# A larger ring of weights in the place of the scratch for GpSimd's transfers

## The chip, the cores and the metric

The kernel runs on one core of a Trainium2 chip. The core has TensorE (PE) for matrix products, VectorE (DVE), ScalarE (ACT) and GpSimd (POOL) for the rest, and SyncE (SP), which here issues the transfers. Weights come from HBM into SBUF, the memory of 128 partitions that the engines read; products go to PSUM. The metric is the time of one execution on the device, in microseconds (us).

## The reference, cut to what matters

Two blocks of two layers each work on 256 tokens of width 1024, all in float32. Each layer is a mixer followed by a mixture of experts. Three of the mixers are attention of one kind or another, the first is a gated MLP beside attention to a memory. The experts are what the change is about:

```python
def hierarchical_moe(h, w_group, b_group, w_expert, b_expert, w_gate, w_up, w_down):
    ...                                   # choice of a group, and of the top two experts in it
    weights = g_w * top_w
    combine = jnp.sum(jax.nn.one_hot(expert_id, N_EXPERTS, dtype=jnp.float32) * weights[..., None], axis=1)
    ...
        gate = jnp.einsum('td,edf->tef', xb, w_gate)
        up = jnp.einsum('td,edf->tef', xb, w_up)
        act = jax.nn.silu(gate) * up * cb[..., None].astype(xb.dtype)
        return jnp.einsum('tef,efd->td', act, w_down)
```

The first two layers have 32 experts, the last two 16, each with 1024 x 256 weights for gate, up and down. `first_block` and `second_block` call this after each mixer, and the second block also scales and shifts by a modulation that is computed from a vector with the weights `w_ada_2`.

## The kernel before, in words

**The ring.** Nearly all weights pass once through one tile, `ring`, of RING columns of float32 (12 MB over the 128 partitions). The whole list of chunks is fixed when the program is built: `Stream.add` gives every chunk its place, wrapping to column 0 where the rest is too short, and works out `need`, the number of earlier chunks that must be used up before it may be overwritten; with LOADS = 16 semaphores for landings, a chunk may also not be issued before the one 16 ahead of it is used. The gate, up and down weights of an expert are three pieces of PIECE = 2048 columns, 1 MB each; those of the dense layers are chunks of 2 or 3 MB, and the 16 chunks of `w_ada_2`, 3 MB each, are spread between them.

**Who fills it.** SyncE alone issues the ring's transfers, in the order of the list (line 96, `Stream.issue`). Each of them waits for `chunk_used`, which the engine that last reads a chunk raises. A block of the program issues what can be freed within it, so the ring runs ahead of the products by as much as it holds. Between them SyncE issues loads that have tiles of their own: the down weights of the first experts of a stage (`first_down`, `half_down`, `hT`, `late_down`, parts of `catT` and `mem_kv`), rows, biases and the router's weights.

**An expert stage (`moe`).** Tokens are sorted by expert with products, and each expert's tokens are taken in a window of 32 slots. Experts are taken in pairs. For a pair i, TensorE computes gate and up in two halves of k (line 1671, 32 products of 128 x 512 each), then the products with the down weights (line 1694), and adds the weighed rows of the pair before (line 1717). GpSimd copies the windows (line 1564), ScalarE applies Silu and frees the ring's pieces (lines 1866, 1868 and 1847), VectorE multiplies and weighs. The order of the ring's pieces is that of `expert_pieces`: gate and up of a pair, then the down weights of the pair before. The down weights of the first 5, 6, 4 and 4 experts (ASIDE) are not in the ring. TensorE waits for a piece where it is first read.

**The general path.** If some expert has more than 32 tokens in one half, every engine branches to code that computes all experts for all tokens (`every_token`). There the combine weights are stored to DRAM and read back, one row per expert, broadcast over the partitions into `cb`.
Of the kernel before, what the change touches and what calls it, by code (L numbers as in the profile page):

```python
# [22 lines left out]
P = 128  # L23
T = 256
# [2 lines left out]
KT = D // P  # L27
EPS = 1e-6
NEG = -1e30
RING = 4 * 6144  # L30
LOADS = 16
FF = 256
PIECE = 2048
# [88 lines left out]
def build(nc, A, out, stop=99):  # L122
    ctx = ExitStack()
    with ctx:
        def sem(name):
            return ctx.enter_context(nc.semaphore(name))
# [3 lines left out]
        def sig(name):  # L130
            if name not in names:
                names[name] = Signal(sem(name))
            return names[name]
# [3 lines left out]
        def sbuf(stack, name, shape, dt=F32):  # L137
            uniq[0] += 1
            return stack.enter_context(nc.sbuf_tensor(f"{name}_{uniq[0]}", shape, dt))
# [12 lines left out]
        PS = ctx.enter_context(nc.psum_tensor("PS", [P, 8, BANK], F32))  # L152
        ring = sbuf(ctx, "ring", [P, RING])
        chunk_used = sem("chunk_used")
# [1205 lines left out]
        def moe(m, first, E, gain, shift, gate, then):  # L1360
# [7 lines left out]
            with ExitStack() as st:  # L1368
# [73 lines left out]
                cb = flat[:, 3072:4096].rearrange("p (j t) -> p j t", j=4)  # L1442
                combT = flat[0:E, 4096:4096 + T]
# [14 lines left out]
                ct_ready, ct_sb, c_stored = sig("combT_ready"), sig("combT_taken"), sig("comb_stored")  # L1458
                gate_ready, up_ready, silu_ready = sig("gate_ready"), sig("up_ready"), sig("silu_ready")
                hid_ready, up_taken = sig("hid_ready"), sig("up_taken")  # L1460
# [7 lines left out]
                cb_loaded = [sig(f"cb_loaded{j}") for j in range(4)]  # L1468
# [51 lines left out]
                def _(pool):  # L1520
# [23 lines left out]
                    def every_token(pool):  # L1544

                        pool.wait_ge(*ct_sb.at(1))
                        nc.gpsimd.dma_start(A["comb_dram"][0:E, :], combT).then_inc(c_stored.sem, 16)
                        pool.wait_ge(*c_stored.at(16))
                        for e in range(E):
                            if e >= 4:  # L1550
                                pool.wait_ge(*up_taken.at(e - 3))
                            nc.gpsimd.dma_start(cb[:, e % 4, :], A["comb_dram"][e:e + 1, :].to_broadcast([P, T])).then_inc(cb_loaded[e % 4].sem, 16)
                        nc.gpsimd.sem_inc(win_ready.sem, 2 * E + 4)

                    far_from_here("gpsimd", f"rows_{m}", block.end_bb, every_token)
                    nc.gpsimd.br_cond(fits(nc.gpsimd) > 0, on_true=f"slots_{m}", on_false=f"rows_{m}")
                    nc.switch_bb(f"slots_{m}")
# [238 lines left out]
                def _(act):  # L1796
# [22 lines left out]
                    def take_ranks_and_weights(act):  # L1819

                        act.wait_ge(*rank_rows.at(1))
                        nc.scalar.copy(ranks, PS[:, 0, 0:T]).then_inc(rank_rows_taken.sem, 1)
                        act.wait_ge(*weight_rows.at(1))
                        nc.scalar.copy(weights, PS[:, 1, 0:T]).then_inc(weight_rows_taken.sem, 1)

                    act.wait_ge(*table_ready.at(1))
                    def every_token(act):

                        take_ranks_and_weights(act)
                        act.wait_ge(*ct_ready.at(1))  # L1830
                        nc.scalar.copy(combT, PS[0:E, 4, 0:T]).then_inc(ct_sb.sem, 1)
                        for e in range(E):
                            act.wait_ge(*gate_ready.at(e + 1))
                            if e >= 2:
                                act.wait_ge(*hid_ready.at(e - 1))
                            nc.scalar.activation(sg[:, e % 2, :], PS[:, 4 + e % 2, :], ACT.Silu).then_inc(silu_ready.sem, 1)
                        nc.scalar.sem_inc(y_high.sem, highs)

                    far_from_here("scalar", f"every_silu_{m}", f"rejoin_act_{m}", every_token)
                    before_branch = nc.cur_bb  # L1840
                    nc.scalar.br_cond(fits(nc.scalar) > 0, on_true=f"silu_{m}", on_false=f"every_silu_{m}")
# [1449 lines left out]
```

## Time and profile before

| | |
|---|---|
| Runs | 1534.68, 1537.2, 1545.22 us; median 1537.2 |
| Profiled execution, its span | 1536.0 us, of 23584 instructions |
| TensorE busy | 1432.1 us, 93% |
| VectorE, ScalarE, GpSimd busy | 737.2, 495.9, 102.6 us |
| Read from HBM | 465.42 MB, 305 GB/s over the span |
| First expert stage, last product pair | 191.6 to 404 us |
| Second | 591.1 to 804 us |
| Third, fourth | 1169.5 to 1266 us, 1432.4 to 1528 us |

The profile is of one execution other than the three that were timed; its span, from the first to the last instruction, is 1.2 us below the median of those. The page is that of the one core. The stretches of the expert stages are read from the timeline of lines 1671 and 1694. The transfers are far from even: 42 to 426 GB/s in the page's 40 slices of 38.4 us.

### The profile page before, as it was taken

To read this page: it belongs to the slowest core of one execution; us is meant where nothing else is said; L and a number is where in the kernel's file an instruction comes from. 1 tells how busy PE (TensorE), PEld (TensorE's weight loads), DVE (VectorE), ACT (ScalarE), POOL (GpSimd) and SP (SyncE) were. 2 spreads that over 40 slices of the span, in tenths; PEclk is the share of its full clock that TensorE was granted. 3 is DMA by queue.
4 is the path that set the end of the run, shared out by engine and by line. 5 is a ranking of instruction groups with operands and counts; after the bars stand their busy time and mean duration, and the time that the engine had idled before them with its cause. 6 is when DMAs were issued, how large, how long until landed. Compare 5 with 4: busy or idle time off the path is not lost. (4 is left out here: it accounts for less than half of the span.)

```text
span 1536.0 us, 23584 instructions
## 1 busy us (share of the span) xinstructions
PE 1432.1 (93%) x9090; PEld 786.3 (51%) x9090; DVE 737.2 (48%) x1659; ACT 495.9 (32%) x996; POOL 102.6 (7%) x258
## 2 busy tenths in 40 slices
PE   7999999987899899998888998999899998989998
PEld 4585533322365644332227876788655336765432
DVE  1467432222255544222226755675585346668534
ACT  3231211111226412111116656565512116661211
POOL 0000011100000001110102000200001102000110
PEclk9999999999999999999999999999898999999999
DMA  8798799999963189999997462335169996437997
GB/s 358 313 365 334 294 381 417 421 420 422 426 266 145 59 336 386 398 422 420 421 424 302 165 225 77 110 143 227 42 230 422 420 425 248 174 156 301 422 420 299
DMA packets 63399, 469.78 MB, mean 306 GB/s; under 512 B 7809, under 2 KB 15921, under 8 KB 18738
## 3 DMA queue, kind: packets, MB, share of 16 engines
q1 hardware_dynamic: 63282, 468.22, 75.2%
q8 instruction: 74, 1.21, 0.3%
q14 instruction: 43, 0.35, 0.1%
HBM read 465.42 MB, written 2.76 MB: 305 GB/s over the span
## 5 line engine op out<-in xcount | busy, mean ns | idle before, releaser
L1671 PE MATMUL PS<-ring,catT 128*32 128x512 f32 x3072 | 348.0, 594 | 18.8 <-issue 16.4
L826 PE MATMUL PS<-w_split,h_split 128*128 128x512 f32 x1152 | 272.7, 396 | 6.0 <-DVE w_split L911 6.0
L826 PEld LDWEIGHTS PS<-w_split,h_split 128*128 128x128 f32 x1152 | 215.5, 190 | 56.9 <-DVE w_split L911 8.5
L1671 PEld LDWEIGHTS PS<-ring,catT 128*32 128x32 f32 x3072 | 96.4, 110 | 235.0 <-issue 234.8
L911 DVE TENSOR_TENSOR w_split<-ring,w_split 128x512 fp32r<-128x512 f32 x192 | 132.6, 705 | 69.3 <-ACT w_split L859 68.7
L1694 PE MATMUL PS<-ring,row_place 128*32 128x512 f32 x1232 | 142.3, 593 | 20.2 <-issue 20.1
L859 ACT CAST w_split<-ring 128x512 fp32r<-128x512 f32 x192 | 118.0, 619 | 106.7 <-PE PS L826 106.2
L1869 ACT ACTIVATE row_place<-PS 128x256 f32<-128x256 f32 x48 | 18.4, 384 | 367.7 <-PE PS L1671 367.7
L1694 PEld LDWEIGHTS PS<-ring,row_place 128*32 128x32 f32 x1232 | 41.4, 110 | 112.1 <-issue 112.1
L508 PE MATMUL PS<-ring,catT 128*128 128x512 f32 x224 | 96.7, 592 | 1.0 <-PEq L1022 1.0
L1564 POOL COPY catT<-xsT 128x256 f32 x176 | 63.3, 404 | 405.4 <-PE PS L1671 397.8
L2054 DVE TENSOR_TENSOR row_place<-PS,row_place 128x256 f32<-128x256 f32 x48 | 20.3, 422 | 132.3 <-ACT row_place L1869 132.3
L2058 DVE COPY row_place<-PS 128x256 f32<-128x256 f32 x48 | 20.4, 424 | 117.4 <-PE PS L1680 117.4
L508 PEld LDWEIGHTS PS<-ring,catT 128*128 128x128 f32 x224 | 42.3, 190 | 53.3 <-issue 53.3
L438 DVE CUSTOM_DVE_ANT_0 ring<-ring,row_place 128x1024 f32<-128x1024 f32 x48 | 55.6, 1223 | 8.5 <-DMA row_place<-silu_dram 5.5
L2079 DVE SCALAR_TENSOR_TENSOR gated_rows<-PS,slot_w,grow 128x512 f32<-128x512 f32 x32 | 24.0, 750 | 68.3 <-PE PS L1694 68.1
L2086 DVE SCALAR_TENSOR_TENSOR xn_split<-PS,slot_w,xn_split 128x512 fp32r<-128x512 f32 x36 | 27.0, 751 | 52.2 <-ACT xn_split L1856 52.2
L1538 POOL MEMSET xsT<- 128x512 f32 x4 | 2.1, 526 | 638.0 <-POOLq L476 510.4
L2601 PE MATMUL PS<-ring,catT 128*128 128x512 f32 x96 | 41.7, 594 | 1.1 <-DVE catT L2493 0.9
L1856 ACT ACTIVATE xn_split<-PS,slot_w 128x512 fp32r<-128x512 f32 x36 | 24.7, 687 | 54.6 <-PE PS L1694 54.6
L438 DVE CUSTOM_DVE_ANT_0 ring<-ring,silu_row 128x1024 f32<-128x1024 f32 x36 | 41.7, 1220 | 1.3 <-PE PS L2400 1.3
L2086 DVE SCALAR_TENSOR_TENSOR xn_low_rows<-PS,slot_w,xn_low_rows 128x512 fp32r<-128x512 f32 x26 | 19.5, 751 | 43.5 <-ACT xn_low_rows L1856 43.5
(445 smaller groups left out, 1869.2 us busy)
## 6 DMA issues: line engine op xcount, KB each, us to landing
ring<-in_moe SPq DMA_DIRECT2D x269, 1024.0 KB, 15.2
ring<-in_w_ada SPq DMA_DIRECT2D x16, 3072.0 KB, 12.2
ring<-in_a_w_in SPq DMA_DIRECT2D x23, 2048.0 KB, 14.4
ring<-in_b_w_in SPq DMA_DIRECT2D x8, 2048.0 KB, 20.1
first_down<-in_moe SPq DMA_DIRECT2D x8, 1024.0 KB, 8.5
ring<-in_a_w_out SPq DMA_DIRECT2D x2, 3072.0 KB, 18.3
ring<-in_b_w_out SPq DMA_DIRECT2D x2, 3072.0 KB, 13.9
ring<-in_w_mem_kv SPq DMA_DIRECT2D x2, 2048.0 KB, 11.5
```

The lines of the kernel that those rows point to most:

```text
L438: last = nc.vector.tensor_tensor_reduce(w[:, m, :], w[:, m, :], row, 1.0, 0.0, ALU.mult, ALU.add, ada_out[:, 6 * c + m:6 * c + m + 1])
L508: last = nc.tensor.matmul(PS[:, i % 8, 0:n], srcT[:, j, t * P:(t + 1) * P], w[:, j, o:o + n], start=j == 0, stop=j == k - 1)
L826: last = nc.tensor.matmul(PS[:, 2 * (i % 2) + t, :], hs[:, hp, k, t * P:(t + 1) * P], wk[:, (KT * i + k) % splits, wp, :], start=k == 0 an ...
L859: nc.scalar.copy(wk[:, (KT * i + k) % splits, 0, :], w[:, k, :]).then_inc(w_high.sem, 1)
L911: nc.vector.tensor_tensor(wk[:, (KT * i + k) % splits, 1, :], w[:, k, :], wk[:, (KT * i + k) % splits, 0, :].bitcast(F32), ALU.subtract).t ...
L1564: nc.gpsimd.tensor_copy(xf[:, i % 2, :, q * HALF:(q + 1) * HALF], padded(q // 2)[:, :, bass.ds(at, HALF)]).then_inc(win_ready.sem, 1)
L1671: last = nc.tensor.matmul(PS[lanes, 4 + i % 2, :].rearrange("p (g f) -> p g f", g=2), xf[:, i % 2, k, lanes], gate_up_weights(2 * i + q % ...
L1694: last = nc.tensor.matmul(PS[lanes, 6 + c, :], hs[:, i % 2, f2, lanes], down_weights(2 * i + q % 2, f2)[:, c * BANK:(c + 1) * BANK], start ...
L1856: nc.scalar.activation(yk(i, 0, c), PS[:, 6 + c, :], ACT.Copy, scale=slot_w[:, i % 2, :]).then_inc(y_high.sem, 1)
L2079: nc.vector.scalar_tensor_tensor(gated[:, c, :], PS[:, 6 + c, :], slot_w[:, i % 2, :], grow[:, c * BANK:(c + 1) * BANK], ALU.mult, ALU.mul ...
L2086: nc.vector.scalar_tensor_tensor(yk(i, 1, c), PS[:, 6 + c, :], slot_w[:, i % 2, :], high, ALU.mult, ALU.subtract).then_inc(y_low.sem, 1)
L2601: last = nc.tensor.matmul(PS[:, bank, :], catT[:, k, t * P:(t + 1) * P], w[:, k, :], start=n == 0, stop=n == 11)
```

## The change

RING grows from 4 x 6144 = 24576 columns to 14 x 2048 = 28672, from 12 to 14 MB. The 16 KB per partition come from the scratch of GpSimd's transfers, which is cut to 64 bytes, and GpSimd issues no transfer any more: the general path's store and its E loads are issued by ScalarE, within its loop over the experts and with the same waits. The ring began at byte 16512 of each partition and begins at byte 192; all tiles behind it move up by 64 bytes.

```diff
--- before.py
+++ after.py
@@ -27,7 +27,7 @@
 KT = D // P
 EPS = 1e-6
 NEG = -1e30
-RING = 4 * 6144
+RING = 14 * 2048
 LOADS = 16
 FF = 256
 PIECE = 2048
@@ -1544,12 +1544,6 @@
                     def every_token(pool):
 
                         pool.wait_ge(*ct_sb.at(1))
-                        nc.gpsimd.dma_start(A["comb_dram"][0:E, :], combT).then_inc(c_stored.sem, 16)
-                        pool.wait_ge(*c_stored.at(16))
-                        for e in range(E):
-                            if e >= 4:
-                                pool.wait_ge(*up_taken.at(e - 3))
-                            nc.gpsimd.dma_start(cb[:, e % 4, :], A["comb_dram"][e:e + 1, :].to_broadcast([P, T])).then_inc(cb_loaded[e % 4].sem, 16)
                         nc.gpsimd.sem_inc(win_ready.sem, 2 * E + 4)
 
                     far_from_here("gpsimd", f"rows_{m}", block.end_bb, every_token)
@@ -1829,7 +1823,13 @@
                         take_ranks_and_weights(act)
                         act.wait_ge(*ct_ready.at(1))
                         nc.scalar.copy(combT, PS[0:E, 4, 0:T]).then_inc(ct_sb.sem, 1)
+                        act.wait_ge(*ct_sb.at(1))
+                        nc.scalar.dma_start(A["comb_dram"][0:E, :], combT).then_inc(c_stored.sem, 16)
+                        act.wait_ge(*c_stored.at(16))
                         for e in range(E):
+                            if e >= 4:
+                                act.wait_ge(*up_taken.at(e - 3))
+                            nc.scalar.dma_start(cb[:, e % 4, :], A["comb_dram"][e:e + 1, :].to_broadcast([P, T])).then_inc(cb_loaded[e % 4].sem, 16)
                             act.wait_ge(*gate_ready.at(e + 1))
                             if e >= 2:
                                 act.wait_ge(*hid_ready.at(e - 1))
@@ -3269,7 +3269,7 @@
     feeds["slot_no"] = np.arange(S2).astype(np.float32)
     feeds["desc"] = np.arange(32, 0, -1).astype(np.float32)
 
-    nc = bacc.Bacc("TRN2", target_bir_lowering=False, num_devices=1)
+    nc = bacc.Bacc("TRN2", target_bir_lowering=False, num_devices=1, dynamic_dma_scratch_size=64)
     A = {"col_at": col_at}
     arrays = {}
     for name, v in feeds.items():
```

The ring's places and needs are worked out when the program is built, so the diff doesn't show what moves. SyncE's queue does. (Rows are: line, operation, destination tile <- source, shape, count; UNCONDITIONAL_BRANCH ends a block; L96 is a transfer into the ring.) Around the start of the first expert stage, the block ahead of it:

```order
@@ -39,5 +39,5 @@
 L254 DMA half_down<-in_moe 128x1024
 L96 DMA ring<-in_a_w_out 128x6144
-L96 DMA ring<-in_moe 128x2048 x12
+L96 DMA ring<-in_moe 128x2048 x14
 L2509 UNCONDITIONAL_BRANCH
 L1502 UNCONDITIONAL_BRANCH
```

and, in the stage itself, behind its own loads:

```order
@@ -45,5 +45,5 @@
 L1508 DMA hT<-in_moe 128x2048
 L1510 DMA late_down<-in_moe 128x2048
-L96 DMA ring<-in_moe 128x2048 x79
+L96 DMA ring<-in_moe 128x2048 x77
 L96 DMA ring<-in_b_w_in 128x4096
 L96 DMA ring<-in_w_ada 128x6144
```

Two pieces of the stage's experts moved from behind the loads of `hT` and `late_down` to ahead of the stage. Around the start of the second expert stage, first the end of the block of the second mixer (L2723), then the block of its output projection:

```order
@@ -58,4 +58,6 @@
 L96 DMA ring<-in_w_ada 128x6144
 L96 DMA ring<-in_b_w_out 128x6144 x2
+L96 DMA ring<-in_w_ada 128x6144
+L96 DMA ring<-in_moe 128x2048
 L2723 UNCONDITIONAL_BRANCH
 L477 UNCONDITIONAL_BRANCH
```

```order
@@ -66,6 +68,5 @@
 L254 DMA half_down<-in_moe 128x1024
 L256 DMA mem_kv<-in_moe 128x2048
-L96 DMA ring<-in_w_ada 128x6144
-L96 DMA ring<-in_moe 128x2048 x6
+L96 DMA ring<-in_moe 128x2048 x7
 L476 UNCONDITIONAL_BRANCH
 L1502 UNCONDITIONAL_BRANCH
```

A 3 MB chunk of `w_ada_2` and the first piece of the experts moved ahead of that projection and of the loads that it begins with; seven pieces follow where six did. The projection ahead of the third expert stage:

```order
@@ -109,23 +109,21 @@
 L485 DMA catT<-in_br 128x20
 L248 DMA first_down<-in_moe 128x2048 x2
-L96 DMA ring<-in_w_ada 128x6144
-L96 DMA ring<-in_moe 128x2048 x2
+L96 DMA ring<-in_moe 128x2048 x6
 L476 UNCONDITIONAL_BRANCH
 L1502 UNCONDITIONAL_BRANCH
-L96 DMA ring<-in_moe 128x2048 x10
+L96 DMA ring<-in_moe 128x2048 x8
 L1508 DMA hT<-in_moe 128x2048
 L1510 DMA late_down<-in_moe 128x2048
-L96 DMA ring<-in_moe 128x2048 x32
+L96 DMA ring<-in_moe 128x2048 x30
 L96 DMA ring<-in_b_w_in 128x4096 x3
 L96 DMA ring<-in_b_w_in 128x128
-L96 DMA ring<-in_b_w_in 128x4096 x2
+L96 DMA ring<-in_b_w_in 128x4096 x3
 L1368 UNCONDITIONAL_BRANCH
 L776 UNCONDITIONAL_BRANCH
-L96 DMA ring<-in_b_w_in 128x4096
 L96 DMA ring<-in_w_ada 128x6144
+L96 DMA ring<-in_b_w_out 128x4096 x2
 L3164 DMA cum_dram<-grow 16x256
 L3167 DMA key_bias<-cum_dram 128x1024 x4
-L96 DMA ring<-in_b_w_out 128x4096 x2
-L96 DMA ring<-in_w_ada 128x6144
+L96 DMA ring<-in_w_ada 128x6144 x2
 L751 UNCONDITIONAL_BRANCH
 L477 UNCONDITIONAL_BRANCH
```

Here too a chunk of `w_ada_2` went to an earlier block, and six pieces of the experts are issued in the place of two.

## Rows read from the trace of the kernel before

**Rows 1.** The page, parts 1 and 2: TensorE's busy time; GB/s by slice.
```profile
PE 1432.1 (93%) x9090; PEld 786.3 (51%) x9090; DVE 737.2 (48%) x1659; ACT 495.9 (32%) x996; POOL 102.6 (7%) x258
...
GB/s 358 313 365 334 294 381 417 421 420 422 426 266 145 59 336 386 398 422 420 421 424 302 165 225 77 110 143 227 42 230 422 420 425 248 174 156 301 422 420 299
```

**Rows 2.** Groups by line, PE, 196 to 300 us: busy and mean | idle before.
```profile
L1671 PE MATMUL PS<-ring,catT 128*32 128x512 f32 x584 | 66.2, 594 | 0.0
L1694 PE MATMUL PS<-ring,row_place 128*32 128x512 f32 x176 | 21.7, 592 | 0.0
```

**Rows 3.** Groups by line, PE, 300 to 400 us.
```profile
L1671 PE MATMUL PS<-ring,catT 128*32 128x512 f32 x412 | 46.9, 594 | 9.4 <-issue 8.5 <-DMA ring<-in_moe 0.9
L1694 PE MATMUL PS<-ring,row_place 128*32 128x512 f32 x226 | 26.3, 595 | 9.5 <-issue 9.5
```

**Rows 4.** Groups by line, PE, 700 to 800 us.
```profile
L1671 PE MATMUL PS<-ring,catT 128*32 128x512 f32 x408 | 46.4, 594 | 9.3 <-issue 7.9 <-DMA ring<-in_moe 1.4
L1694 PE MATMUL PS<-ring,row_place 128*32 128x512 f32 x232 | 26.8, 595 | 9.5 <-issue 9.5
```

**Rows 5.** Stretches: length, busy by engine (x), PEclk, DMA share, GB/s.
```profile
135.00:141.00 6.00, 6.00 (x15) 2.65 (x14) 5.85 (x12) 0.23 (x1) 0.00 (x0) 1.00 1.04 428
185.00:196.00 11.00, 10.84 (x90) 6.54 (x90) 9.39 (x32) 4.94 (x11) 3.36 (x12) 1.00 0.28 95
196.00:300.00 104.00, 104.00 (x928) 33.65 (x928) 29.32 (x74) 15.10 (x27) 13.46 (x38) 1.00 1.00 410
300.00:400.00 100.00, 81.12 (x700) 26.36 (x693) 21.48 (x51) 12.30 (x21) 7.18 (x20) 1.00 1.01 422
430.00:530.00 100.00, 93.33 (x423) 63.80 (x423) 58.61 (x146) 48.07 (x136) 0.00 (x0) 0.98 0.37 148
700.00:800.00 100.00, 81.18 (x702) 26.46 (x698) 21.93 (x52) 12.31 (x21) 7.19 (x20) 1.00 1.01 422
1177.00:1182.00 5.00, 5.00 (x50) 1.45 (x46) 0.82 (x3) 0.38 (x1) 1.44 (x4) 1.00 1.02 418
```

**Rows 6.** Timeline, PE, 270 to 345 us: start, length, what [idle before].
```profile
275.22 3.64 PE L1671 MATMUL PS<-ring,catT 128*32 128x512 f32 x32
...
287.16 3.64 PE L1671 MATMUL PS<-ring,catT 128*32 128x512 f32 x32
...
314.05 3.64 PE L1671 MATMUL PS<-ring,catT 128*32 128x512 f32 x32
...
328.99 3.64 PE L1671 MATMUL PS<-ring,catT 128*32 128x512 f32 x32
```

**Rows 7.** The page, part 6: issues, KB each, us to landing.
```profile
ring<-in_moe SPq DMA_DIRECT2D x269, 1024.0 KB, 15.2
```

**Rows 8.** Timeline, SP queue, 164 to 197 us.
```profile
169.88 1.28 SPq L96 DMA_DIRECT2D ring<-in_moe  x3
...
178.46 0.33 SPq L1508 DMA_DIRECT2D hT<-in_moe  x1
191.73 0.33 SPq L1510 DMA_DIRECT2D late_down<-in_moe  x1
196.39 1.42 SPq L96 DMA_DIRECT2D ring<-in_moe  x2
```

**Rows 9.** Timeline, PE, ends of the third and fourth expert stages.
```profile
1253.10 3.64 PE L1671 MATMUL PS<-ring,catT 128*32 128x512 f32 x32
...
1261.75 3.64 PE L1694 MATMUL PS<-ring,row_place 128*32 128x512 f32 x32 [0.81 <-issue]
...
1515.94 3.64 PE L1671 MATMUL PS<-ring,catT 128*32 128x512 f32 x32
...
1523.86 3.64 PE L1694 MATMUL PS<-ring,row_place 128*32 128x512 f32 x32 [0.33 <-issue]
```

**Rows 10.** Waits of the SP queue: total us, times, longest.
```profile
SPq L2723 <- PEq L2723: 26.3, 1, 26.3
```

**Rows 11.** The page, part 5: GpSimd's copies of windows.
```profile
L1564 POOL COPY catT<-xsT 128x256 f32 x176 | 63.3, 404 | 405.4 <-PE PS L1671 397.8
```

## The prediction

> **What bounds the kernel now.** I read the page first, for the whole span: TensorE is busy for 1432.1 of 1536.0 us, and the row of GB/s says that the transfers run in bursts, 420 and more in some slices, 42 to 145 in others [rows 1]. So there is no single bound, and the change has to be priced stage by stage. The two kinds of bursts that matter are the expert stages, where every expert's weights (3 pieces of 1 MB) pass through the ring.
>
> The groups by line for two halves of the first expert stage come next. From 196 to 300 us the products of gate and up (L1671) and of the down weights (L1694) have 0.0 us of idle time before them [rows 2]; from 300 to 400 us the same two lines have 9.4 + 9.5 = 18.9 us of it [rows 3]. The second expert stage repeats this: 9.3 + 9.5 = 18.8 us from 700 to 800 us [rows 4]. The table by stretch shows what runs meanwhile: from 300 to 400 us the DMA share is 1.01 at 422 GB/s and TensorE is busy for 81.12 of 100 us, from 700 to 800 us 81.18 of 100 [rows 5]. The rows name "issue" as the releaser for most of this, but the period gives the cause away. A pair of experts takes TensorE 287.16 - 275.22 = 11.94 us while nothing is missing, and 328.99 - 314.05 = 14.94 us later [rows 6]. A piece is 1024 KB [rows 7], 1.0486 MB; at 422 GB/s that is 2.485 us, and the six pieces of a pair take 14.9 us. That is the late period: in the second half TensorE waits for weights.
>
> The picture is thus a race. TensorE eats a pair in 11.94 us, the transfers bring one in 14.9 us, and the stage starts with a full ring of 12 pieces as a head start. It lasts until about 300 us; from then to the end of the stage the last piece's landing sets the time.
>
> **What the change does to the race.** The ring holds 14 pieces. The rows of the order show it for SyncE: 14 pieces of the first expert stage stand ahead of that stage's other work where 12 stood, and 77 behind where 79 stood; for the second stage one piece moves into an earlier block, 7 + 6 instead of 6 + 6 follow, and 76 stand behind where 78 stood.
>
> Step 1: are the two more pieces there in time? They cost 2 x 2.485 = 4.97 us of transfer, ahead of the stage. Before the first stage SyncE issues three ring pieces at 169.88 us and then none until 196.39 us, when the first slot comes free [rows 8]; from 185 to 196 us the DMA share is 0.28 [rows 5], that is 0.72 x 11 = 7.9 us of idle transfer time, and 4.97 fits. Before the second stage the share is 0.37 in the 100 us from 430 to 530 us, into which the order moves one 3 MB and one 1 MB transfer [rows 5]. So yes, in both.
>
> Step 2: does the later stream keep its pace? A slot is freed by the same products at the same times while TensorE does not wait, so piece n+2 goes out when piece n did, and everything that the stage brings lands two pieces, 4.97 us, earlier. TensorE has 18.9 and 18.8 us of such waiting to give back, more than 4.97, so the whole of it comes through: **4.97 us in each of the two long stages, 9.94 together**. Nothing downstream takes it back: the transfers of the next stage follow in the same queue and move up by the same 4.97 us.
>
> Step 3: the two short expert stages (16 experts). Here the head start lasts almost to the end. From the start of the last gate and up half to the start of the last down products it is 1261.75 - 1253.10 = 8.65 us in the third, 1523.86 - 1515.94 = 7.92 us in the fourth, with a last wait of 0.81 and 0.33 us [rows 9]. The third gives back at least the 0.73 us by which it is the longer, at most 1.04 with the 0.33 that the fourth waits too; the fourth gives 0 to 0.33. I take 0.9 and 0.1, since a chain through ScalarE and VectorE stands before those products in any case: **1.0 us**.
>
> Step 4: what is moved past what. SyncE's queue is in order. In the block of the second mixer it now waits for a further slot before it reaches the block's end; it stood there for 26.3 us before the others came [rows 10], so 0. In the first expert stage the load for `hT` and the one for `late_down` go out at 178.46 and 191.73 us [rows 8], now behind up to 4.97 us more of transfers; the products that read `hT` are the second pair's down products, behind a whole pair of 11.94 us, and those that read `late_down` one pair later, so 0. Before the third stage a 3 MB load of `w_ada_2` moves ahead of its block; VectorE had hardly waited for it: 0, at most a few tenths gained.
>
> Step 5: the general path. It does not run here: GpSimd's copies of windows, x176 in L1564, are those of the short path [rows 11]. The 1 + E transfers that move to ScalarE cost nothing, and neither does the lost scratch, as no transfer of this execution is issued by GpSimd. If an input did take that path, ScalarE would wait for a store and for `up_taken` ahead of its Silu; no row prices that.
>
> **The sum.** 4.97 + 4.97 + 1.0 = 10.9 us. The profiled execution spans 1536.0 us, so its successor spans 1525.1. The median of the three runs, 1537.2, lies 1.2 us above that span, and what surrounds it is not touched: **1526.3 us**, 0.7% less. The bounds of the terms give 9.9 to 11.3 us, 1525.9 to 1527.3.
>
> The price of a piece deserves a second look, as all hangs on it: the row gives 422 GB/s [rows 5], hence 2.485 us. The Trainium skill, "DMA: Bandwidth & Descriptors", Specifications, lists a limit of about 358 GB/s for one core's share of HBM; by that (an estimate from the page) a piece would take 2.93 us and the sum would be 12.7 us, 1524.5. The measured rate decides, and it is above that limit.
>
> **Rivals.**
>
> *The dips go too (faster).* In the first halves of the long stages the rate is 410 GB/s, not 422 [rows 5]. Should the deeper ring close that, it is worth (1 - 410/422) x 104 = 3.0 us in each, some 5.7 more: 1520.6. Against it: the rate dips where all free slots have been filled, and slots come free at TensorE's pace whatever the ring's size. Chance 0.07.
>
> *Part of the head start does not come through.* A piece may land late, or the chain behind the products may already be the bound once waits are shorter. Then one piece's worth or nothing is gained in each stage: 1531 to 1537. Against it: the 7.9 us of idle time, and 0.0 us of idle in [rows 2]. Chance 0.10.
>
> *The transfers get slower (the other side).* The ring moves in SBUF: it began at byte 16512 of a partition (128 above a multiple of 256) and now begins at byte 192 (192 above one), and all tiles behind it shift by 64 bytes. In a long stage 77 pieces, 191 us, follow the first free slot; a rate lower by 2.6% eats the 4.97 us, and anything above makes the kernel slower. At 7% each long stage would lose 13.4 - 5.0 = 8.4 us, 1554. Against it: from 135 to 141 us, when mostly `first_down` and `half_down` are filled (both 160 above a multiple of 256), the rate is 428 GB/s, no less than in the ring [rows 5]. Chance 0.03.
>
> *A mild form of it.* From 1177 to 1182 us, when the third stage's `hT` and `late_down` are filled, the rate is 418 GB/s, 1% below 422 [rows 5]. If the ring fell to that, each long stage would lose 1.9 us: 1526.3 + 3.8 = 1530.1. Chance 0.08, for the same reason. The Trainium skill, "DMA: Bandwidth & Descriptors", section "How a descriptor splits into AXI transactions", has a rule of that size: an estimate from it is that a row of 8192 bytes starting 128 above a boundary of 256 costs 260 beats and one starting 192 above it 262, 0.8% more, if the written side follows it too. By that rule the time would be 1529.4; the 428 GB/s of the other tiles speaks against it so far.
>
> *The ring does not grow in effect.* 16 semaphores count the landings, and a piece may be issued only when that of 16 before is used. 14 pieces stay below that, and the order shows them ahead of the stage. I give it no chance.
>
> **Chances and range.** Forecast 0.72, the rivals 0.07, 0.10, 0.03, 0.08. I call 1% what a measurement can tell from no change; 1% of 1537.2 is 15.4 us. Faster by more needs the dips to go, or a favourable spread: 0.09. Slower by more is the strong form of the third rival: 0.03. Within 1%: 0.88. The runs of before spread from 1534.68 to 1545.22, so the median itself may sit 2 or 3 us off; with the first rival below and the mild one and half of the second above, the range is 1520 to 1533.
>
> **What would show it.** In the changed kernel's trace: SyncE's issues ahead of the first expert stage x14; the first long stage's waits in L1671 and L1694 begin one to two pairs later than 300 us and sum to about 14 us instead of 19; the pair's late period stays 14.9 us and the rate 422 GB/s; the last down products of that stage start 5 us earlier against its own start; from the last gate and up half to the last down products the third stage takes 7.9 us or less. I am wrong if the rate in the late halves is not 421 to 423 GB/s, if the head start's two pieces land after the stage's first slot comes free, or if the stages between gain or lose more than 1 us.

## The result, and the profile after

The first four runs of the changed kernel took 1514.16, 1522.96, 1509.48 and 1518.09 us, median 1516.12; the ratio to the kernel before is 0.9887 [0.9851, 0.9924]. Six more runs beside other kernels gave 1512.75 us and 0.9863 [0.9837, 0.9888]. So the change makes the kernel 1.1 to 1.4% faster, 17 to 21 us; 10.9 us were forecast, and 1516.12 lies below the range of 1520 to 1533. Two executions far above the others, one of 1849.55 us of the kernel before and one of 3552.27 us of e1 below, are left out throughout as slow ones.

The profiled execution spans 1512.4 us, 23.6 us less than the one before. First its page: busy times, granted clock and transfer rate in 40 slices, and the issues of ring pieces. They answer to [rows 1, 7].

```profile
span 1512.4 us, 23584 instructions
PE 1419.4 (94%) x9090; PEld 776.4 (51%) x9090; DVE 736.8 (49%) x1659; ACT 495.6 (33%) x996; POOL 102.5 (7%) x258
...
PEclk9999999999999999999999999999899999999999
...
GB/s 360 362 346 254 419 343 413 420 421 420 427 300 188 112 279 419 402 421 420 420 425 285 187 291 44 111 158 221 68 261 421 420 423 300 173 107 302 421 419 239
...
ring<-in_moe SPq DMA_DIRECT2D x269, 1024.0 KB, 13.8
```

The work is the same; TensorE's busy time fell by 12.7 us although it does the same products. That can't come from waits that are gone, and the mean granted clock of the execution, in the view of the cores, says what it is, before and after.

```profile
core: us from the first to the last instruction, mean granted TensorE clock
core 0: 1536.0 us, clock 0.975
```
```profile
core: us from the first to the last instruction, mean granted TensorE clock
core 0: 1512.4 us, clock 0.985
```

Next the waits, as groups by line of PE over the whole of the first long stage (192 to 399 us) and of the second (581 to 786 us), after. The columns are those of [rows 2].

```profile
L1665 PE MATMUL PS<-ring,catT 128*32 128x512 f32 x1024 | 116.1, 594 | 6.8 <-issue 6.1 <-DMA ring<-in_moe 0.7
L1688 PE MATMUL PS<-ring,row_place 128*32 128x512 f32 x432 | 51.0, 593 | 6.9 <-issue 6.9
...
L1665 PE MATMUL PS<-ring,catT 128*32 128x512 f32 x1024 | 116.0, 594 | 6.2 <-issue 5.3 <-DMA ring<-in_moe 0.9
L1688 PE MATMUL PS<-ring,row_place 128*32 128x512 f32 x416 | 47.4, 593 | 6.3 <-issue 6.3
```

The waits sum to 13.7 and 12.5 us, where 18.9 and 18.8 stood [rows 3, 4]. The stages themselves, from the first product of gate and up to the last down product, stand in the tables by stretch: before, then after, then the three stretches between the stages of either. The columns are those of [rows 5].

```profile
191.63:403.62 211.99, 193.11 (x1699) 62.89 (x1698) 56.05 (x142) 30.16 (x53) 22.64 (x64) 1.00 1.00 413
591.14:803.14 212.00, 193.18 (x1699) 62.95 (x1698) 55.70 (x142) 30.16 (x53) 22.64 (x64) 1.00 1.00 411
1169.53:1265.39 95.86, 95.00 (x850) 30.73 (x850) 38.09 (x95) 15.14 (x29) 11.13 (x32) 1.00 1.02 422
1432.39:1527.49 95.10, 94.76 (x850) 30.74 (x850) 37.83 (x95) 15.16 (x29) 11.18 (x32) 1.00 0.96 397
403.62:591.14 187.52, 177.97 (x713) 109.40 (x711) 95.57 (x234) 65.77 (x171) 1.90 (x6) 0.96 0.59 241
803.14:1169.53 366.39, 341.52 (x1826) 267.14 (x1826) 234.91 (x443) 198.54 (x379) 17.51 (x22) 0.94 0.48 183
1265.39:1432.39 167.00, 155.05 (x785) 109.63 (x786) 121.34 (x303) 89.33 (x194) 9.63 (x14) 0.96 0.59 236
```
```profile
192.40:398.48 206.08, 192.42 (x1699) 62.64 (x1698) 56.00 (x142) 30.17 (x53) 22.59 (x64) 1.00 1.00 412
581.06:785.83 204.77, 192.23 (x1699) 62.48 (x1698) 55.66 (x142) 30.16 (x53) 22.60 (x64) 1.00 1.01 417
1148.99:1243.57 94.58, 94.58 (x850) 30.66 (x850) 37.82 (x94) 15.00 (x29) 11.12 (x32) 1.00 1.01 421
1408.34:1502.92 94.58, 94.58 (x850) 30.66 (x850) 37.86 (x94) 15.01 (x29) 11.11 (x32) 1.00 0.91 378
398.48:581.06 182.58, 171.28 (x711) 104.58 (x711) 95.51 (x234) 65.65 (x171) 1.89 (x6) 1.00 0.62 255
785.83:1148.99 363.16, 338.62 (x1826) 264.19 (x1826) 234.63 (x443) 198.49 (x379) 17.57 (x22) 0.95 0.52 196
1243.57:1408.34 164.77, 152.84 (x786) 108.17 (x786) 121.51 (x303) 89.33 (x195) 9.74 (x14) 0.98 0.60 237
```

The four stages give 5.9, 7.2, 1.3 and 0.5 us, 14.9 together. Between them 4.9, 3.2 and 2.2 us more are gone, with the granted clock (the seventh column) up from 0.96 to 1.00, from 0.94 to 0.95 and from 0.96 to 0.98. It is busy time alone that fell there: TensorE stands idle for 9.55, 24.87 and 11.95 us before and for 11.30, 24.54 and 11.93 after. Two questions follow: how much of 14.9 us is the ring and how much the luck of two executions, and why the clock is higher.

The steps that need only the trace: from 300 to 398 us and from 685 to 785 us the rate is as it was [rows 5], and the late pairs keep their period (319.31 to 334.51 is 15.2 us, with one landing 0.3 us late in it), here from the timeline of PE.

```profile
300.00:398.00 98.00, 84.34 (x734) 27.32 (x726) 22.91 (x54) 13.00 (x22) 7.16 (x20) 1.00 1.02 422
...
685.00:785.00 100.00, 87.46 (x760) 28.64 (x756) 24.00 (x59) 13.01 (x22) 7.16 (x20) 1.00 1.01 422
```
```profile
319.31 3.64 PE L1665 MATMUL PS<-ring,catT 128*32 128x512 f32 x32 [0.47 <-issue]
...
334.51 3.64 PE L1665 MATMUL PS<-ring,catT 128*32 128x512 f32 x32 [1.64 <-issue]
```

### The profile page after: what moved, and what is told of

It reads as the page before. It is cut to its first block and busy times, and to the rows that moved or that the text cites. A ratio compares the mean times of both kernels' runs of the same rounds, so it can differ in the third digit from the quotient of the medians.

```text
span 1512.4 us, 23584 instructions
## 1 busy us (share of the span) xinstructions
PE 1419.4 (94%) x9090; PEld 776.4 (51%) x9090; DVE 736.8 (49%) x1659; ACT 495.6 (33%) x996; POOL 102.5 (7%) x258
## 5 line engine op out<-in xcount | busy, mean ns | idle before, releaser
L1869 ACT ACTIVATE row_place<-PS 128x256 f32<-128x256 f32 x48 | 18.5, 384 | 361.1 <-PE PS L1665 361.1
L791 POOL TENSOR_TENSOR h_split<-hT,h_split 128x256 fp32r<-128x256 f32 x24 | 23.7, 995 | 235.8 <-ACT h_split L869 233.1
## 6 DMA issues: line engine op xcount, KB each, us to landing
ring<-in_a_w_in SPq DMA_DIRECT2D x23, 2048.0 KB, 10.9
ring<-in_w_mem_kv SPq DMA_DIRECT2D x2, 2048.0 KB, 11.3
```

## The experiments

Two figures are used throughout. A kernel's **mean granted clock** is the mean over its timed runs. Its time **at equal clock** is from one straight line through 186 runs of 15 kernels (all but the ring of 10 pieces), with a level of its own for each: 10.3 us (standard error 0.5) per 0.01 of clock, read at 0.980. It leaves 2.1 us of scatter where the plain times of one kernel scatter by 2 to 6.

### Only the depth, undone and in steps

```diff
-RING = 14 * 2048
+RING = 12 * 2048        # e1; 13 * 2048 in e2, 10 * 2048 in e4
```

> The changed kernel with its ring back at 12 pieces: the missing scratch, the ring's new address and ScalarE's issues stay, and only the depth is undone. Theory, the depth is all of it: the four expert stages are as long as in the kernel before (212.0, 212.0, 95.9 and 95.1 us, within 1 us of the landing stalls' scatter), and the ratio to the kernel before is 0.998 to 1.002. Rival, the layout does something (address or scratch): the ratio stays below 0.995 and transfers in the late halves are faster than 2.485 us a piece. Rival, the clock: the part of the difference outside the expert stages (8.7 us of 23.6 in the two profiled executions, nine stretches of low granted clock instead of thirteen) is scatter; then this kernel's executions show both kinds of profile, low ones near 9 and near 13.

Measured: 1535.34 us, ratio 0.9995 [0.9966, 1.0023]. The address of the ring, the missing scratch and ScalarE's issues do nothing that these runs can tell (0.3% at most); the depth is all of it. This falsifies both rivals of slower transfers as well: the ring lies at its new place here too, and the time at equal clock is 1533.7 us, that of the kernel before. The clock was 0.9795, that of the kernel before (0.9792 in 75 runs), and its trace has twelve low stretches: the clock did not rise with the rest of the change.

> A ring of 13 pieces, all else as in the changed kernel. Theory, depth: one piece of 2.485 us in each long stage, so about 209.5 us for each, and in the third stage nearly all of what 14 give (94.6 to 95.0 us); the ratio lies halfway between that of 12 and of 14 pieces, about 0.995. Rival, something that comes with the change as a whole and not per piece: the ratio is that of 14 pieces, 0.989, or that of 12.

Measured: 1528.57 us, ratio 0.9952 [0.9925, 0.9979]; at equal clock 1526.0 against 1533.7, so 7.7 us for the first piece and 7.0 for the second. The long stages took 208.41 and 209.72 us, as expected; the third 96.27, not 94.6 to 95.0, in this one execution. Its queue had issued the last burst 18.3 us ahead of that stage, and the piece for the first freed slot landed 18.0 us into it; the section on the third stage tells what that does.

```diff
+HELD = 12 * 2048
+            held = i
+            while held and sum(hi - lo for lo, hi in self.place[held - 1:]) <= HELD:
+                held -= 1
-            self.need.append(max([0, i - len(self.loaded) + 1, *self.need[-1:], *behind]))
+            self.need.append(max([0, i - len(self.loaded) + 1, *self.need[-1:], *behind, held]))
```

> The ring has 14 pieces of room, but a transfer is issued only while at most 12 pieces are in it. Theory, what counts is how many pieces are ahead of TensorE: long stages of 212 us, ratio to the kernel before 0.998 to 1.002, as with 12 pieces of room. Rival, what counts is that a slot is written later after it was read, or which addresses are written: ratio 0.989 as with 14.

Measured: 1529.56 us, ratio 0.9962 [0.9937, 0.9986]. The long stages took 211.56 and 211.12 us, so there the theory holds. But the two short ones took 94.58 us each, no wait in them, as with 14 pieces of room. That was not expected: the same 12 MB were worth more in a ring of 14. The stretch of its third stage:

```profile
1165.24:1259.82 94.58, 94.58 (x850) 30.66 (x850) 37.86 (x94) 15.00 (x29) 11.11 (x32) 1.00 1.01 421
```

The cause is in SyncE's rows ahead of the third stage, below.

> A ring of 10 pieces. Theory, depth: the waits begin two pairs earlier, each long stage takes 5.0 us more than with 12 pieces (217 us), and the two short ones, in which the head start of 12 just about lasts, take 4 to 5 us more each (about 100 us). Sum 18 to 20 us, ratio 1.012 to 1.013. Rival, there is a loss beside the head start as the ring shrinks (transfers between the stages come late too, as some stages keep 3 MB transfers in it): over 1.015. Rival, the head start is worth less than its bytes: under 1.008.

Measured: 1622.03 us, ratio 1.0584 [1.0540, 1.0627], a plain miss of the theory; the first rival, a loss beside the head start, had been put at over 1.015. The long stages took 215.65 and 214.66 us and the short ones 101.71 and 99.24, near the forecast, 19.0 us above e1 in all. The other 68 us were lost elsewhere. Against the trace of e1, 18.8 us of them lie ahead of the first stage and 9.9, 13.0 and 21.4 us between the stages; the granted clock was lower too, 0.9588 in the mean. A later kernel narrows down the reason:

> Room for 14 pieces, but the pieces of the expert stages are held at 10 in the ring; the 2 and 3 MB transfers of the other stages are free to use all 14. Theory, the 87 us that the ring of 10 pieces lost were not head start but the large transfers, which leave gaps at the end of a ring of 10 MB and wait for each other: here the parts between the expert stages are as long as with 12 (184 and 367 us, not 194 and 381), the long stages take 212 + 5 = 217 us, less what the ring of 10 showed (215 us), the short ones 99 to 101; ratio 1.006 to 1.012. Rival, the ring of 10 was slow because so few pieces are in flight in an expert stage: ratio above 1.03.

Here ring pieces of the expert stages are held at 10 as above, and nothing else. Measured: 1546.42 us, ratio 1.0099 [1.0062, 1.0137], with 215.5, 215.2, 98.7 and 100.3 us in the stages. The tables by stretch for the part between the first and second stage and for that between the second and third, the ring of 10 ahead of the held one:

```profile
426.74:620.88 194.14, 175.65 (x711) 106.96 (x711) 95.66 (x234) 65.83 (x172) 1.89 (x6) 0.96 0.55 222
835.54:1216.35 380.81, 339.65 (x1825) 265.49 (x1826) 235.28 (x443) 198.42 (x379) 17.59 (x22) 0.94 0.46 173
```
```profile
407.44:596.61 189.17, 177.94 (x710) 108.41 (x710) 95.51 (x234) 65.62 (x171) 1.90 (x6) 0.96 0.57 232
811.81:1171.33 359.52, 334.96 (x1825) 260.62 (x1826) 235.00 (x443) 198.52 (x379) 18.29 (x22) 0.96 0.50 187
```

With the room of 14 TensorE stands idle for 11.2 and 24.6 us in them, as in the other kernels (9.6 and 24.9 in e1, 11.3 and 24.5 after); in the ring of 10 for 18.5 and 41.2. So what the ring of 10 lacked was room for the transfers of the other stages, a second effect of a ring's size. That it is the way in which they fit (ten pieces hold three transfers of 3 MB and leave 1 MB unused), and not the smaller room as such, is inferred; no run separates the two. In the expert stages a piece less costs about what was forecast: 4.3 to 4.8 us for two in each long one.

### The third stage

The timeline of SyncE's queue ahead of the third stage, in the kernel before, in e3, and after:

```profile
1128.02 0.33 SPq L96 DMA_DIRECT2D ring<-in_w_ada  x1
1135.91 17.62 SPq L96 DMA_DIRECT2D ring<-in_moe  x12
...
1169.53 0.33 SPq L1510 DMA_DIRECT2D late_down<-in_moe  x1
```
```profile
1126.59 0.33 SPq L100 DMA_DIRECT2D ring<-in_w_ada  x1
1126.96 24.16 SPq L100 DMA_DIRECT2D ring<-in_moe  x12
...
1165.24 0.33 SPq L1514 DMA_DIRECT2D late_down<-in_moe  x1
```
```profile
1110.51 24.24 SPq L96 DMA_DIRECT2D ring<-in_moe  x14
...
1148.99 0.33 SPq L1510 DMA_DIRECT2D late_down<-in_moe  x1
```

`late_down` goes out as the stage begins. Before, the first piece goes out 33.6 us ahead of it, behind the 3 MB transfer of `w_ada_2`; in e3 38.3 us ahead, in the changed kernel 38.5. The output projection ahead of the stage begins at 1118.60, 1117.29 and 1101.10 us (its first product in the timeline of PE), and each queue goes on 9.3 to 9.4 us behind that. The ring of 12 then has room for the `w_ada_2` transfer alone, and the first piece goes out 7.9 us later; with 14 MB of room, in e3 as in the changed kernel, pieces go out at once. What they gain is transfer time, not only room. From the DMA rows of 50 us (40 before the stage, 10 of it; 40 slices) of the kernel before and after:

```profile
GB/s 157 413 393 452 452 367 190 406 426 426 197 20 0 13 0 26 203 413 419 439 426 426 433 419 419 433 419 419 419 419 419 426 419 433 426 413 433 419 419 406
```
```profile
GB/s 20 33 170 406 426 433 433 426 439 426 439 419 419 419 144 13 0 0 170 406 419 433 426 419 426 426 419 419 426 439 419 426 419 419 413 419 426 419 426 406
```

Before the pause both move weights; after it both are at the limit without a break into the stage. So this short stage is bound by transfers from the start on. The first slot comes free 4.8 us into every stage. In the long stages of the changed kernel the ring is full by then (its last piece landed 4.6 us ahead of the first stage and 1.8 us into the second); in the third stage of the kernel before it is not, its last piece landed 7.4 us into the stage. The piece for the first freed slot landed 15.3 us into the third stage before, 12.6 after and 12.5 in e3, against 10.5 us into the first stage before and 9.6 after. With 12 pieces the length of the third stage depends on how long ahead of it the burst behind the pause is issued. Two further traces with 12 pieces (e9 and e11, below) show what that does: third stages of 99.01 and 98.60 us. Its stretch by engine, and the stretch from the issue of the burst to the stage's start, e9; then the latter in the kernel before:

```profile
1159.30:1258.31 99.01, 95.42 (x850) 30.93 (x850) 38.09 (x95) 15.15 (x29) 11.08 (x32) 1.00 1.01 421
...
1141.48:1159.30 17.82, 17.74 (x114) 15.74 (x115) 15.13 (x50) 9.06 (x17) 1.79 (x6) 0.81 0.95 387
```
```profile
1148.48:1169.53 21.05, 20.96 (x114) 18.44 (x114) 14.85 (x50) 9.07 (x17) 1.81 (x6) 0.68 0.96 393
```

The same 114 products took 21.05 us at a clock of 0.68 and 17.82 at 0.81. The faster clock brings the stage 3.2 us nearer to the burst, and the stage gives 3.2 us back in waits (99.01 - 95.86). The other two traces agree: 21.1 us and a stage of 95.88 in e1, 18.3 us and 98.60 in e11, so that the two sum to 116.8 to 117.0 us in all four. With 14 pieces the third stage was 94.58 or 94.59 us in all six traces, whatever the clock ahead of it.

### What the waits of the long stages are

```diff
+            n = PIECE // 2 if self.raw(i).shape[1] == PIECE and i >= 29 else self.raw(i).shape[1]
-            nc.sync.dma_start(self.raw(i), self.chunks[i])
+            nc.sync.dma_start(self.raw(i)[:, 0:n], self.chunks[i][:, 0:n])
```

> The changed kernel in which the transfers of the expert stages bring half of each piece (from the 15th piece of the first stage on), so that half of the products read what was in the slot before; the number of transfers, waits and products is the same. Theory, the late waits are transfer time: all of TensorE's waits in the two long stages are gone (13.7 and 12.5 us), the stages take 192.4 us each, and the ratio to the kernel before is about 0.974 (1520 - 26 us). Rival, part of these waits is a chain through the other engines or the queue (a wait seen by TensorE, but not for bytes): the long stages stay above 196 us.

The kernel leaves out the second half of each piece, and the products read what lay in the slot before; it serves as a measurement alone. Measured: 1491.0 us, ratio 0.9724 [0.9690, 0.9757]; the long stages took 190.27 us each. The table by stretch:

```profile
194.20:384.47 190.27, 190.27 (x1699) 61.43 (x1698) 56.06 (x142) 30.12 (x53) 22.63 (x64) 1.00 0.76 258
566.42:756.69 190.27, 190.27 (x1699) 61.40 (x1698) 55.70 (x142) 30.14 (x53) 22.64 (x64) 1.00 0.76 265
```

No idle time is left, at the same number of transfers. The waits named "issue" were bytes, and 30.3 us are still in reach in the changed kernel's two long stages (206.08 + 204.77 - 2 x 190.27: 26.2 us of waits, the rest in what TensorE is busy around them).

### Where the higher clock comes from

> The changed kernel once more, unchanged, for a larger sample and a second trace. At equal granted clock the runs so far put 12 pieces of room at 1533.7 and 1534.3 us, 13 at 1526.0, and 14 at 1520.0 from four runs only. Theory, the rest was chance: the mean clock of twelve runs is 0.980 as in the other kernels (0.9837 in the four), the median is 1519 to 1521, the ratio 0.990 to 0.992, the long stages 206 to 207 us, and some of the low-clock stretches missing from the first trace are back. Rival, fewer waits raise the clock: the mean clock stays at 0.983 or more and the ratio at 0.989. Rival, the stalls in the early half of the second stage (4.5 to 5.9 us in three traces with 12 pieces, 4.8 with 13, 2.2 with 14) go with the deeper ring: they are about 2 us again; by chance alone they are back at 5.

Measured: 1512.75 us, ratio 0.9863 [0.9837, 0.9888], mean clock 0.9858. Chance as the cause of the higher clock falls: the ten runs of the changed kernel have 0.985 in the mean, and the 26 runs of 14 pieces other than e12 0.9847, against 0.9792 in 75 of the kernel before. (The stalls of the second stage's early half were 5.0 us again, against 2.2 in the first trace; here chance is at work.) "Fewer waits raise it" falls too, since e6 waits least of all and has 0.9778. The remaining runs move the program in time, with fillers on TensorE:

```diff
-                    keep_busy(3, 12)
+                    keep_busy(3, 12 + 8 if m == 0 else 12)    # e8, e9; 4 in e10, e11
+                    keep_busy(3, 12 + 8 if m == 2 else 12)    # e12; m == 1 in e13, e14 and, with 4, e15
```

> The changed kernel with eight more filler products of TensorE (0.21 us each, 1.7 us) ahead of the first expert stage's gathering products; everything behind them stands 1.7 us later. The ten runs of the changed kernel have a mean granted clock of 0.985, 39 runs of the kernel before 0.9797; that is 5 us of the difference. Theory, alignment: the low-clock stretches stand at the same places of the program in every trace, and whether each falls, and how long it is, depends on how the program's pauses lie in time; the 13 to 15 us by which 14 pieces move the later parts happen to suit them. Then a shift of 1.7 us changes the mean clock (down toward 0.980), and the time grows by more than 1.7 us. Rival, the clock is higher because TensorE's waits in the expert stages are fewer: the mean clock stays at 0.985, and the time grows by 1.7 us.

> The kernel before with the same eight filler products. Theory, alignment: its mean clock changes too, and since it is low (0.9797), more likely up than down, so that the time grows by less than 1.7 us or falls. Rival, waits: the clock stays at 0.980 and the ratio to the kernel before is 1.001.

> The changed kernel with four more filler products, 0.85 us. Theory, alignment: a mean clock between those of no shift and of 1.7 us, or outside both. Rival, waits: 0.985 and 0.85 us more than the changed kernel.

> The kernel before with four more filler products, 0.85 us. Theory, alignment: its mean clock differs from 0.9797 by more than its standard error. Rival, waits: it does not. At equal clock both shifted kernels of 12 pieces and both of 14 keep the distance of 14.8 us that the rows show so far.

> The changed kernel with eight more filler products (1.7 us) ahead of the third expert stage's gathering products, so that what lies behind that stage stands as late against the stage before it as with 12 pieces, whose third stage is 1.3 us or more longer. In all four traces of 14 pieces no stretch of low clock falls 95 us behind the third stage, in all four of 12 pieces one does. Theory, alignment: that stretch is back in the trace, the mean clock goes from 0.984 to 0.981 or below, and the time rises by 3 to 6 us. Rival, it goes with 14 pieces as such: clock 0.984, time 1.7 us more than the changed kernel (1514), the stretch stays absent.

> The changed kernel with the eight filler products ahead of the second expert stage. Theory, alignment: the landing stalls of the second stage scatter its end by about 1 us anyway, so that this shift does little, like the one ahead of the first stage: clock 0.983 to 0.985. Rival: the same clock; this run by itself only bounds how much a shift there can do.

> The kernel with half the bytes in the expert stages (half of the products read what was in the slot before), with eight more filler products ahead of the second expert stage. Theory, alignment: its clock, 0.977 to 0.980 in four runs, moves by more than 0.003 in one direction. Rival, the clock is set by what the kernel does and not by where it lies: 0.978 again, the time 1.7 us above the 1490 us without them.

> The same with four filler products (0.85 us). Theory, alignment: the clock differs from that with none and with eight. Rival: 0.978 again, the time 0.85 us above 1490 us.

| kernel | shift | median us | ratio | mean clock | at 0.980 |
|---|---|---|---|---|---|
| before (75 runs) | | | | 0.9792 | 1533.7 |
| e1, 12 pieces | none | 1535.34 | 0.9995 | 0.9795 | 1533.7 |
| e11, 12 pieces | 0.85 us, first stage | 1535.99 | 1.0004 [0.9978, 1.0029] | 0.9773 | 1533.7 |
| e9, 12 pieces | 1.7 us, first | 1537.29 | 1.0013 [0.9991, 1.0036] | 0.9791 | 1536.2 |
| changed, and e5 | none | 1516.12, 1512.75 | 0.9887, 0.9863 | 0.9837, 0.9858 | 1520.0, 1518.3 |
| e10, 14 pieces | 0.85 us, first | 1513.51 | 0.9866 [0.9834, 0.9897] | 0.9840 | 1518.6 |
| e8, 14 pieces | 1.7 us, first | 1516.16 | 0.9863 [0.9832, 0.9894] | 0.9842 | 1519.8 |
| e13, 14 pieces | 1.7 us, second | 1513.80 | 0.9861 [0.9828, 0.9893] | 0.9855 | 1520.0 |
| e12, 14 pieces | 1.7 us, third | 1522.01 | 0.9909 [0.9878, 0.9940] | 0.9795 | 1520.3 |
| e6, half bytes | none | 1491.0 | 0.9724 | 0.9778 | 1487.8 |
| e15, half bytes | 0.85 us, second | 1482.56 | 0.9660 [0.9629, 0.9691] | 0.9824 | 1486.6 |
| e14, half bytes | 1.7 us, second | 1486.15 | 0.9665 [0.9635, 0.9696] | 0.9814 | 1486.8 |

The shifts ahead of the first stage change the clock of neither ring, which is what the rival of the alignment theory had forecast for e8 to e11, and the one ahead of the second (e13) does nothing either. With the one ahead of the third stage the clock of 14 pieces is back at that of 12: 1.7 us of fillers there cost 7.0 us in the mean of eight runs (1520.9 against 1513.8). In the kernel with half the bytes the fillers go with a faster program, 1485.3 and 1484.1 us in the mean against 1490.1; these are five, five and four runs whose times overlap, so this is a hint and not a result.

One detail of the forecast failed, and it is the one that would have tied the loss to a place: in the trace of e12 (clock 0.981, one of its better runs) the stretch of low clock 95 us behind the third stage was not back. The part between the third and the fourth stage, in e1, after and e12:

```profile
1261.34:1428.40 167.06, 155.04 (x787) 109.70 (x787) 121.34 (x303) 89.31 (x194) 9.61 (x14) 0.96 0.60 237
...
1243.57:1408.34 164.77, 152.84 (x786) 108.17 (x786) 121.51 (x303) 89.33 (x195) 9.74 (x14) 0.98 0.60 237
...
1247.11:1411.56 164.45, 151.68 (x786) 107.03 (x786) 121.49 (x303) 89.34 (x195) 9.62 (x14) 0.98 0.59 237
```

This part took 164.4 to 164.9 us in all six traces with 14 pieces and 167.0 to 172.8 in the four with 12: 4.0 us in the mean. The part between the second and the third stage gives another 4.0 (364.6 against 360.6, e12 with its fillers aside). But that between the first and the second took 185.6 us in the mean with 12 and 184.9 with 14 (e13 aside), so most of the 4.9 us that the two profiled executions differ by there was luck. What is shown, then, is that the higher clock comes with the depth (e1 has all else), that fewer waits are not what raises it (e6), and that a shift ahead of the third stage takes it away. That it depends on how the late parts lie in time is the reading that fits these best; no trace shows where e12 lost its 7 us.

That stretch shows the dependence best. By table of stretches, the 8 us ahead of it and its 3.4 us, before and after:

```profile
1353.00:1361.00 8.00, 5.51 (x42) 3.02 (x42) 4.64 (x27) 5.35 (x18) 0.00 (x0) 1.00 0.60 257
1361.00:1364.40 3.40, 3.40 (x19) 2.00 (x17) 1.84 (x11) 2.50 (x11) 0.00 (x0) 0.50 0.01 2
```
```profile
1331.00:1339.00 8.00, 5.58 (x46) 3.39 (x46) 5.33 (x31) 5.58 (x19) 0.00 (x0) 1.00 0.80 343
1339.00:1342.40 3.40, 3.40 (x32) 2.13 (x30) 3.11 (x20) 3.40 (x12) 0.00 (x0) 1.00 0.01 2
```

Same place, same products, the same two pauses of 1.03 and 1.46 us ahead of it (the stretches of after are set 0.7 us later against the second pause, hence the other counts in the first of the two); before, 2.4 GHz fell to 1.2 for 3.4 us, 0.3 us behind that pause, and after it did not. What exactly decides it I leave open; it was not isolated further than by the shifts.

## Why the prediction was wrong, step by step

**The forecast's time fails by three terms**; the mechanism, its steps 1, 2 and 5, stands.

*The price per piece in the long stages* (4.97 us each): right. Four traces with 12 pieces in effect (before, e1, e9, e11) have 211.1 and 211.4 us in the mean, six with 14 (after, e5, e8, e10, e12, e13) 206.5 and 205.3: 4.6 and 6.0 us, 10.7 for the 9.94 forecast. A single late landing is worth about 1 us and there are several in each stage, so the 5.9 and 7.2 us of the two profiled executions were partly luck. The pieces were there in time (the last of the 14 landed 4.6 us ahead of the first stage, and the piece for the first freed slot 9.6 us into it, 10.5 before), the late rate is 422 GB/s, and the first wait of the first stage comes 126.9 us into it instead of 112.4, a pair and a bit later.

*Step 3, the short stages* (1.0 us): wrong, and it is the term of the mechanism that failed. I read the third stage as one whose "head start lasts almost to the end", from one execution's last wait. In truth its transfers were behind from the start, and its waits were small only as a stretch of low clock had held the stage back. Over the same traces it took 97.3 us with 12 pieces and 94.6 with 14, the fourth 94.9 and 94.6: 2.7 + 0.3 = 3.0 us, not 1.0. The one trace of e3 has the whole gain of the third stage with 12 pieces held, so that it needs the room beside the 3 MB transfer and not 14 pieces ahead. The edit that step 4 put at nothing "or a few tenths", the 3 MB load of `w_ada_2` ahead of its block, belongs to this. The sign that I had named for it, 7.9 us or less from the last gate and up half to the last down half, was met (1232.56 to some 1239.9 us) and was too weak to tell 1.0 from 3.0. (Small sums of the forecast are off as well: 0.73 + 0.33 is 1.06 and not 1.04, its own least value of 0.73 puts the lower bound of the sum at 10.7 and not 9.9, and twice 3.0 is 5.9 or 6.0 and not 5.7. None of them matters here.)

The stages together give 10.7 + 3.0 = 13.7 us, and the comparison at equal clock 14.7 (1533.7 - 1519.0, standard error about 0.9): they agree.

*The clock* was no term at all. I wrote that stages between may gain or lose 1 us at most, or I am wrong; they gained 4.9, 3.2 and 2.2. The clock went from 0.9792 to 0.985, and 0.0058 x 10.3 us per 0.01 is 6.0 us. That this comes with the depth is shown (e1); that the cause is how the later parts lie in time, for which the mean clock of e12 speaks, is not.

*The base.* 1537.2 was the median of three runs; 75 later ones have a mean of 1534.5. That is 2.7 us of the miss. Then 1534.5 - 13.7 - 6.0 = 1514.8; the ten runs have a mean of 1513.8.

*Rivals.* Both slower forms died with e1 and with 422 GB/s; e1 has the new address and the old time. The rule of the Trainium skill ("DMA: Bandwidth & Descriptors", "How a descriptor splits into AXI transactions"), from which I had estimated a loss of 0.8%, shows in no run here: with the ring at either address a piece lands every 2.48 to 2.50 us in the late halves of the long stages, where 0.8% would be 0.02 us. "The dips go too" did not happen: from 196 to 300 us the rate is 408 GB/s (410 before), and the second stage's stalls came back in e5. "Part of the head start does not come through" did not happen either. No queue moves cost anything (step 4), and the general path did not run (step 5).

## What to carry to other kernels

Where a stream through a ring bounds the end of a stage, one more slot is worth about one slot's transfer time in each such stage, as long as there is idle transfer time ahead of it to fill the slot; look at the landings behind the stage's start, not only at the last wait, to see which stages those are, and at how the largest transfer fits into the ring. Where TensorE pauses often, a change can gain or lose 6 us in 1500 by the granted clock beside what it is made for: compare clocks of many runs before a small rest is explained by the mechanism, and take the base from more than three.

## What the runs showed of the hardware

A stage that is bound by transfers from its start turns a faster clock ahead of it into waits: 3.2 us gained by the clock and 3.2 us lost in the third stage. A small change of schedule can change the mean granted clock: with 1.7 us of fillers ahead of the third stage it was 0.9795 in place of 0.985, and the kernel took 7.0 us more. That fillers can also gain time (the half-byte kernel) is a hint from few runs.

In a busy stream of 1 MB transfers, 76 to 79 in a long stage, one to five land 0.4 to 2.9 us late. Their places are not all chance: in all 14 traces with whole pieces, one to three of them fall 46 to 61 us into the second long stage. Late landings are also much more frequent where SyncE has little queued. Counted over the two long stages of these traces, of the pieces issued 2 to 5 us before the landing ahead of them 37 of 143 came more than 0.4 us late, of those issued 10 us or more before it 31 of 1460. Why a transfer is late at all, nothing in the traces says.
